# Half of the convolution's taps on GpSimd, root-mean-square norms by quarters, the last expert block written out

## What is computed

```python
a_lat = modulate(rms_norm(h_lat, g_pre_t), sh_t, sc_t)          # the same for ctx
z = split_columns(a @ w_in)                                      # conv, q, kv, k_rope, gmlp, gate
u = a_ * sigmoid(gate); u = depthwise_conv(u, dw, 31 taps) + db  # CONV_DIM = 512 channels
br_conv = silu(layer_norm(u)) @ w_conv_out
br_attn = attention(q, k, v) @ w_attn_out                        # 8 heads, 96 channels each
br_gmlp = chunk_gmlp(z_gmlp) @ w_gmlp_out
y = (g_conv * br_conv + g_attn * br_attn + g_gmlp * br_gmlp) @ w_out
h = h + gt_t * rms_norm(y, g_post_t)
f = swiglu(...)                      # layer 0: dense, width 2816
f = moe_swiglu(...)                  # layer 1: 8 experts of width 3584, top 2, 256 tokens
h = h + gt_f * rms_norm(f, g_post_f)
```

## Time and profile before

| | us |
|---|---|
| median of three runs | 2535.28 (2527.91 to 2539.51) |
| profiled execution | 2527.79, its span 2526.0 |
| blocks in the loop | 9, some 123.4 us each |

### The profile page before, as it was taken

One profiled execution on the slowest core, in us unless ns is written; L12 is line 12 of the kernel. 1 busy time (PEld: TensorE's weight loads), 2 busy tenths in 40 slices (PEclk: granted clock), 3 DMA queues, 4 the chain that ended last, 5 costly groups with the idle time before them and its releaser, 6 DMA issues.

```text
span 2526.0 us, 32159 instructions
## 1 busy us (share of the span) xinstructions
PE 2401.4 (95%) x12058; PEld 1943.0 (77%) x12058; DVE 1754.8 (69%) x1806; ACT 1385.4 (55%) x1455; POOL 46.0 (2%) x87
## 2 busy tenths in 40 slices
PE   7999999998999998877997999999999999999997
PEld 4757778875787885766996788888888888888886
DVE  4569753426333335778666989898989888888886
ACT  3456443334222223564656677777777777767675
POOL 0011000001000000000000000000000000000000
PEclk9989999999999999998998999999999999999998
DMA  7245223345434333313573999999999998989994
GB/s 278 73 133 188 67 84 109 109 162 197 134 109 134 108 99 126 105 38 105 167 250 139 371 346 368 354 355 360 360 349 367 348 367 340 376 338 373 341 373 175
DMA packets 104679, 579.36 MB, mean 229 GB/s; under 512 B 11920, under 2 KB 13840, under 8 KB 54800
## 3 DMA queue, kind: packets, MB, share of 16 engines
q1 hardware_dynamic: 93072, 536.21, 57.6%
q0 software_dynamic: 11520, 41.95, 4.8%
HBM read 577.06 MB, written 1.05 MB: 229 GB/s over the span
## 4 chain that ended last, share of the span: by engine, by line
PE 86%; DVE 8%; ACT 3%; issue 2%; DMA 1%; SPq 0%; DVEq 0%; ACTq 0%
PE bank L616 25%; PE bank L617 25%; PE bank L618 25%; DVE cacc L1549 2%; PE bank L691 2%; PE bank L1000 1%; PE bank L789 1%; DVE rstd L1490 1%; PE bank L1065 1%; PE bank L809 1%; PE bank L666 1%; DVE wlo L1470 1%; DVE t L1505 1%; ACT whi L1113 1%; DMA mod_s<-in_mod 1%
## 5 line engine op out<-in xcount | busy, mean ns | idle before, releaser
L1771 DVE TENSOR_TENSOR elo<-eraw,ehi 128x2048 fp32r<-128x2048 f32 x388 | 884.7, 2287 | 136.4 <-ACT ehi L1159 135.3
L1159 ACT CAST ehi<-eraw 128x2048 fp32r<-128x2048 f32 x388 | 741.2, 1914 | 254.0 <-PE bank L618 250.0
L1470 DVE TENSOR_TENSOR wlo<-raw,whi 128x1024 fp32r<-128x1024 f32 x220 | 269.5, 1225 | 286.8 <-ACT whi L1113 285.3
L616 PE MATMUL bank<-ah,whi 128*128 128x512 f32 (+1 forms) x1088 | 396.9, 365 | 19.7 <-DVE al L1511 9.3
L616 PE MATMUL bank<-ehi,xgh 128*128 128x512 f32 x1024 | 405.8, 396 | 1.5 <-DVE xgl L1777 1.2
L617 PE MATMUL bank<-elo,xgh 128*128 128x512 f32 x1024 | 399.7, 390 | 0.0
L618 PE MATMUL bank<-ehi,xgl 128*128 128x512 f32 x1024 | 399.3, 390 | 0.0
L617 PE MATMUL bank<-al,whi 128*128 128x512 f32 (+1 forms) x1088 | 390.0, 358 | 0.0
L618 PE MATMUL bank<-ah,wlo 128*128 128x512 f32 (+1 forms) x1088 | 389.9, 358 | 0.0
L1113 ACT CAST whi<-raw 128x1024 fp32r<-128x1024 f32 x220 | 229.2, 1042 | 118.9 <-PE bank L618 118.8
L616 PEld LDWEIGHTS bank<-ah,whi 128*128 128x128 f32 x1088 | 208.5, 192 | 57.5 <-issue 17.8
(11 more groups left out here) (270 smaller groups left out, 2766.2 us busy)
## 6 DMA issues: line engine op xcount, KB each, us to landing
eraw<-in_moe SPq DMA_DIRECT2D x388, 1024.0 KB, 4.9
raw<-in_dense SPq DMA_DIRECT2D x220, 512.0 KB, 3.5
mod_b<-in_mod POOLq DMA_DIRECT2D x48, 512.0 KB, 5.0
mod_a<-in_mod POOLq DMA_DIRECT2D x32, 512.0 KB, 4.3
mod_s<-in_mod SPq DMA_DIRECT2D x16, 512.0 KB, 12.9
hres<-in_xT SPq DMA_DIRECT2D x1, 2048.0 KB, 8.1
wsT<-in_wsT SPq DMA_DIRECT2D x2, 512.0 KB, 3.5
out_h<-hres SPq DMA_DIRECT2D x2, 512.0 KB, 3.0
```

The source lines that it names most:

```text
L616: pe.matmul(dst, wh, xh, start=first, stop=False, skip_group_check=True)
L1159: nc.scalar.copy(ehi[c % ESPLIT][:], eraw[c % ERAW][:]).then_inc(e_hi, 1)
L1470: dve.tensor_tensor(wlo[c % SPLIT][:], raw[c % RAW][:], whi[c % SPLIT][:].bitcast(F32), ALU.subtract).then_inc(w_lo, 1)
L1771: dve.tensor_tensor(elo[c % ESPLIT][:], eraw[c % ERAW][:], ehi[c % ESPLIT][:].bitcast(F32), ALU.subtract).then_inc(e_lo, 1)
```

## The change

**Taps.** The channel tiles 2 and 3 move to GpSimd, in both layers. For each tap it makes the product of the shifted input and the tap in a tile `tapp` and adds it to `cacc`: product 2, product 3, addition 2, addition 3. `tapp` lies over a part that `uk` and `uv` read, so from the second tap on it waits for `uv`. VectorE keeps tiles 0 and 1, one tap a unit in layer 0 and two in layer 1. PE waits for each half's sums by their own semaphore. GpSimd's loads of `mod_a` move to SyncE.

**Norms.** `add_squares` makes four matmuls of 32 output rows, each over a quarter of the tokens, so the sums lie in 32 rows each and 128 (or 64) columns; root and reciprocal work on these; `spread_roots` brings them by four matmuls with one column of `sel8` into the 128 rows and 512 columns of a PSUM bank `RB`, from which the multiplications read. The norms over the query, key and value channels, the convolution and the gMLP stay as they were.

**Experts.** The loop runs `n_iter` - 1 times on every engine; the last block follows as straight code without gather, `a` and `g` of q = 7, and without the splits and loads for them and for what would follow.

The core of the diff; the same replacements at the other norms, and the loop bodies of ScalarE and VectorE, which become functions in the same way, are left out:

```diff
@@ tables
+DVE_TILES = 2
 TAPS_CA = (5, 5, 5, 5)
-TAPS_UNIT = (2, 3)
+TAPS_UNIT = (1, 2)
+LAST_STEPS = [_s for _s in STEPS if _s[0] != "gather" and not (_s[0] in ("a", "g") and _s[1] == NB)]
+LAST_CHUNKS = [(*_s, _p) for _s in LAST_STEPS for _p in range(parts_of(_s[0]))]
@@ places
+        tapp = place("tapp", [P, 2, 2, LAT], F32, gm0 + 10240)
-        niter_i = place("niter_i", [P, 1], I32)
+        niter_i = place("niter_i", [P, 2], I32)
@@ sync
+                if c == CHUNK[("uk", 0)]:
+                    sp.wait_ge(mod_used, MOD_START)
+                    for i in range(MOD_A):
+                        sp.dma_start(mod_a[i][:], A["mod"][MOD_START + i]).then_inc(moda_landed[i], 16)
+                if c == CHUNK[("gv", 0, 2)]:
+
+                    for i in range(MOD_A, (VECS - 2) * KD):
+                        sp.wait_ge(mod_used, MOD_START + i - MOD_A + 1)
+                        sp.dma_start(mod_a[i % MOD_A][:], A["mod"][MOD_START + i]
+                                     ).then_inc(moda_landed[i % MOD_A], 16)
 ...
-            n_iter = sp.value_load(niter_i[0:1, 0:1], min_val=BLOCKS_MIN, max_val=BLOCKS_MAX)
-            with sp.Fori(0, n_iter) as it:
+            n_last = sp.value_load(niter_i[0:1, 1:2], min_val=BLOCKS_MIN - 1, max_val=BLOCKS_MAX - 1)
+            with sp.Fori(0, n_last) as it:
 ...
-            sp.wait_ge(e_lo, n_iter * EN + (EPRE + ERAW))
+            this = sp.value_load(ids_i[0:1, bass.ds(n_last, 1)], min_val=0, max_val=EXPERTS - 1)
+            for m in range(ERAW, EN_LAST):
+                sp.wait_ge(e_lo, n_last * EN + (EPRE + m - ERAW + 1))
+                fetch(A["moe"][bass.ds(this, 1)], stored(ECHUNKS.index(LAST_CHUNKS[m])), EPRE + m)
+
+            sp.wait_ge(e_lo, n_last * EN + (EPRE + EN_LAST))
@@ gpsimd
-            for i in range((VECS - 2) * KD):
-                pool.wait_ge(mod_used, MOD_START + max(i - MOD_A + 1, 0))
-                pool.dma_start(mod_a[i % MOD_A][:], A["mod"][MOD_START + i]).then_inc(moda_landed[i % MOD_A], 16)
+            tap_made = [0]
+
+            def taps(L):
+
+                ns = live(L) // LAT
+
+                def acc(i):
+                    return cacc[:, i, 0:ns * LAT].rearrange("p (s t) -> p s t", s=ns)
+
+                def product(t, i):
+                    src = up[:, i, 0:ns, t:t + LAT]
+                    w = p_(L, "conv_dw", TAPS * i + t)
+                    if t == 0:
+                        taken(pool, ("ca", L, i))
+                        pool.tensor_scalar(acc(i), src, w, p_(L, "conv_db", i), ALU.mult, ALU.add
+                                           ).then_inc(tap_done[i], 1)
+                    else:
+                        if (t, i) == (1, DVE_TILES):
+                            pool.wait_ge(chunk_used, CHUNK[("uv", L)] + 1)
+                        pool.wait_ge(tap_done[i], (TAPS - 1) * L + t)
+                        pool.tensor_scalar(tapp[:, i % 2, 0:ns, :], src, w, None, ALU.mult).then_inc(tap_made_sem, 1)
+                        tap_made[0] += 1
+
+                def addition(t, i, made):
+                    pool.wait_ge(tap_made_sem, made)
+                    pool.tensor_tensor(acc(i), acc(i), tapp[:, i % 2, 0:ns, :], ALU.add
+                                       ).then_inc(tap_done[i] if t < TAPS - 1 else conv_sum_pool, 1)
+
+                for t in range(TAPS):
+                    made = {}
+                    for i in range(DVE_TILES, 4):
+                        product(t, i)
+                        made[i] = tap_made[0]
+                    if t:
+                        for i in range(DVE_TILES, 4):
+                            addition(t, i, made[i])
+
+            taps(0)
 ...
+            taps(1)
@@ tensor
+            def add_squares(x, ntok, first, last):
+
+                w = ntok // 4
+                for j in range(4):
+                    mm = pe.matmul(STAT[32 * j:32 * j + 32, 0:w], ones[:, 0:32], x[:, j * w:(j + 1) * w],
+                                   start=first, stop=last, skip_group_check=True)
+                return mm
+
+            def spread_roots(ntok):
+
+                w = ntok // 4
+                pe.wait_ge(rs_ready, n.next(rs_ready))
+                for j in range(4):
+                    mm = pe.matmul(RB[:, j * w:(j + 1) * w], sel8[:, 2 * j:2 * j + 1].broadcast_to([P, P]),
+                                   rstd[:, 0:w], start=True, stop=True, skip_group_check=True)
+                mm.then_inc(rb_psum, 1)
 ...
                     for k in range(KD):
                         mod_chunk()
+                        if k == KD // 2:
+                            spread_roots(TOK)
                     stat_bank()
                     for k in range(KD):
                         pe.wait_ge(sq_ready, n.next(sq_ready))
-                        mm = pe.matmul(STAT[:], ones[:], t16[:, k, :], start=(k == 0), stop=(k == KD - 1),
-                                       skip_group_check=True)
+                        mm = add_squares(t16[:, k, :], TOK, k == 0, k == KD - 1)
                         if k == KD - 1:
                             mm.then_inc(sumsq_psum, 1)
                         mod_chunk()
                     n.next(sumsq_psum)
+                    spread_roots(TOK)
 ...
-                    pe.wait_ge(conv_sum, 4 * L + k + 1)
+                    if k < DVE_TILES:
+                        pe.wait_ge(conv_sum, DVE_TILES * L + k + 1)
+                    else:
+                        pe.wait_ge(conv_sum_pool, (4 - DVE_TILES) * L + k - DVE_TILES + 1)
 ...
-            with pe.Fori(0, n_iter) as it:
+            def iteration(it, steps):
                 c = EPRE
-                for kind, q, half in STEPS:
+                for kind, q, half in steps:
 ...
+            with pe.Fori(0, n_last) as it:
+                iteration(it, STEPS)
+            iteration(n_last, LAST_STEPS)
@@ scalar
+            def root_quarters(ntok):
+                w = ntok // 4
+                act.wait_ge(sumsq_psum, n.next(sumsq_psum))
+                nc.scalar.activation(std[:, 0:w], STAT[:, 0:w], ACT.Sqrt, bias=eps[:, 0:1], scale=1.0 / D
+                                     ).then_inc(std_ready, 1)
 ...
+            def round_next(it, c, steps):
+                if steps is STEPS or c < EPRE + EN_LAST:
+                    round_e(it, c)
@@ vector
+            def invert_quarters(ntok):
+
+                dve.wait_ge(std_ready, n.next(std_ready))
+                dve.reciprocal(rstd[:, 0:ntok // 4], std[:, 0:ntok // 4]).then_inc(rs_ready, 1)
+                dve.wait_ge(rb_psum, n.next(rb_psum))
 ...
-                    chain(dve.tensor_tensor(y[:, k, 0:ntok], y[:, k, 0:ntok], rstd[:, 0:ntok], ALU.mult))
+                    chain(dve.tensor_tensor(y[:, k, 0:ntok], y[:, k, 0:ntok], RB[:, 0:ntok], ALU.mult))
 ...
-                    taps_left.append([L, i, 0])
+                    if i < DVE_TILES:
+                        taps_left.append([L, i, 0])
 ...
-            dve.tensor_copy(niter_i[:], before[:, 16:17]).then_inc(niter_ready, 1)
+            chain(dve.tensor_copy(niter_i[:, 0:1], before[:, 16:17]))
+            dve.tensor_scalar(niter_i[:, 1:2], before[:, 16:17], 1.0, None, ALU.subtract).then_inc(niter_ready, 1)
```

More of the change, by code:

```diff
@@ L100 @@
 EN = 6 * NB
+EN_LAST = len(LAST_CHUNKS)
 ERAW = 6
@@ L659, in stat_bank, with sum_squares @@
                     pe.wait_ge(std_ready, n.n[sumsq_psum])
-            def sum_squares(nk, src, ntok):
-                stat_bank()
+            def add_squares(x, ntok, first, last):
[11 more added lines that the diff above has]
+                mm.then_inc(rb_psum, 1)
+            def sum_squares(nk, src, ntok, quarters=False):
+                stat_bank()
+                if quarters:
+                    for k in range(nk):
+                        pe.wait_ge(sq_ready, n.next(sq_ready))
+                        mm = add_squares(src(k), ntok, k == 0, k == nk - 1)
+                    mm.then_inc(sumsq_psum, 1)
+                    n.next(sumsq_psum)
+                    return
                 for k in range(nk):
@@ L1175, in _ @@
                     copy_rows(0)
-                    root(TOK, 1.0 / D, 0)
+                    root_quarters(TOK)
                     copy_rows(1)
@@ L1343, in _ @@
                 n.next(ysq_used, 1)
-                root(nq, 1.0 / D, 0)
+                root_quarters(nq)
                 if L:
@@ L1424, in _, with iteration @@
             n_iter = act.value_load(niter_i[0:1, 0:1], min_val=BLOCKS_MIN, max_val=BLOCKS_MAX)
-            with act.Fori(0, n_iter) as it:
+            n_last = act.value_load(niter_i[0:1, 1:2], min_val=BLOCKS_MIN - 1, max_val=BLOCKS_MAX - 1)
+            def round_next(it, c, steps):
+                if steps is STEPS or c < EPRE + EN_LAST:
+                    round_e(it, c)
+            def iteration(it, steps):
                 c = EPRE
-                for kind, q, half in STEPS:
+                for kind, q, half in steps:
                     if (kind, half) == ("scatter", 1):
```

(9 more changed lines are left out.)

70 lines of the change are left out of this document (43 added, 27 removed).

## The result

| | before | changed |
|---|---|---|
| median of five runs, us | 2535.28 (2527.91 to 2539.51) | 2546.87 (2546.43 to 2549.60) |
| profiled execution, span | 2526.0 | 2547.8 |

The changed kernel is slower by half a per cent: ratio 1.0053, 95% interval 1.0033 to 1.0073. I had forecast 2507, which is faster. Rival (b), GpSimd at the slower bound, said 2549.

What follows compares the result with a forecast made beforehand. TensorE, busy 95%, was taken as the bound, so cuts pay where it does less or stands. Norms -18.0, last block -16.2, taps +6 gave -28: 2500 us profiled, 2507 as median; range 2470 to 2560.

Steps and rivals of the forecast that it cites:

- Rival (b): Convolution taps: GpSimd at its slower bound, a pair 2.45 us, done at 334 and 1201; total 2549 us; chance 0.18.
- norms: Quarter norms in the layers and at the start: shorter sums, roots and reciprocals, less added spreading; -18.0 us, from -10 to -23.
- last block: Ninth expert block written out, without gather, dead products and unused weight split: -16.2 us, from -10 to -18.
- taps: Convolution taps moved to GpSimd: done at 304 in layer 0 and 1188 in layer 1, together +6 us.
- the price of GpSimd's pair: One tap's product and addition on GpSimd: 1.95 us at 512 columns, bounds 1.3 and 2.65; 1.18 at 256.
- The turns: VectorE's two-SBUF-operand instructions exclude GpSimd's for their whole length, all added to GpSimd: 42 us layer 0, 29 layer 1.
- fewer taps: VectorE's row beside GpSimd: the saving from its fewer taps, 0.7 us a unit, is eaten by its turns of waiting.
- bare norms: Four 512-token norms, at the end of layer 0's mixer and between the layers: -1.8 us each, together -7.2.
- The sums in PE's row: Layer 0's output projection and last feed-forward group: seven sums of squares each, 14 x 0.52 = 7.3 us saved.
- Layer 1's two norms at 256 tokens: Layer 1's norm chains: -0.3 us each, -0.6 together; seven sums there save another 0.9.
- the start: Eight squares at the kernel's start shrink by some 5 us, weights may still be landing: -2 taken, between 0 and -5.
- the uncovered turn: Last expert block: transpose, copies and hand-overs ahead of the last down-projections, 2.1 us instead of 11.6, giving -9.5.

Runs made afterwards that it cites:

- experiment 1: The changed kernel with all taps back on VectorE, quarter norms and written-out last block kept: 2498.31 us, ratio 0.9866 to the kernel before.
- experiment 3: The kernel before with only the last expert block written out: 2518.92 us, ratio 0.9946 to the kernel before.
- experiment 6: The changed kernel with GpSimd's product written as product and addition of constant 0: 2506.55 us, ratio 0.9883 to the kernel before.
- experiment 4: The changed kernel with VectorE's taps 1 to 29 of each of its two tiles left out: 2395.36 us, with eight expert blocks instead of nine.
- experiment 2: The changed kernel with one channel tile on GpSimd instead of two, VectorE at two and three taps a unit: 2518.74 us, ratio 0.9936 to the kernel before.
- experiment 7: The changed kernel with one tile on GpSimd instead of two, VectorE at one and two taps a unit: 2505.28 us, ratio 0.9884 to the kernel before.
- experiment 5: As experiment 4, but GpSimd's product in layer 0 changes its form every five taps; product 1.55 us, with addition of zero 0.69; no total time given.
- experiment 10: Experiment 1 with 16 of 31 taps of one layer 1 tile on GpSimd, cheap form, behind attention: 2500.35 us, ratio 0.9861 to the kernel before.

## Why the prediction was wrong

| term of the sum | forecast | measured |
|---|---|---|
| norms | -18.0 | -12.9 by the fixed points (experiment 1), some -20 by medians |
| last block | -16.2 | -17.2 (experiment 3), -17.9 (experiment 1), some -14 by medians |
| taps | +6 | +52.6 by the fixed points, some +47 by medians |
| sum | -28 | +21.8 between the two traces, +11.6 between the medians |

Two of the three terms held. **The step that failed is the price of GpSimd's pair.** I bounded it from a memset by the number of streams, 1.3 to 2.65 us, and took 1.95. Alone it is 2.77, outside the 1.7 to 2.2 that the prediction allowed itself (0.91 + 0.70 = 1.61 at 256 columns, where the upper bound was 1.5). The addition, 1.23, was near my 1.10; the product, with fewer streams, was the dear one, 1.54 for 0.85. A bound by streams can't see that a form of an instruction has a price of its own. The forecast's middle fits a form that the change doesn't use, 0.69 + 1.24 = 1.93, and with it experiment 6 came to 2507, the forecast. That is luck in part, since the forecast held no loss in attention. Since 0.1 us a pair is 6 us in layer 0, the error of 0.82 is 49 us there.

**The turns** were costed at their full length, 42 us in layer 0, all of it on GpSimd. GpSimd took 188 us from 144.7 to 332.7, 22 more than 60 x 2.77 (12 of them by VectorE's taps, experiment 4), and VectorE's taps in that stretch grew by 42 x 0.27 = 11. So the exclusion that the Trainium skill states ("SBUF — State Buffer", section "Who interferes with whom") shows in kind, but GpSimd paid about half of the length that I had put on it, and a part fell on VectorE. That part I had called eaten by fewer taps. It is not: it stands on the path ahead of each query. With GpSimd at work beside them layer 1's scores took 11 to 14 us more in the traces of experiments 2, 4, 6 and 7 and of the changed kernel (20 in experiment 5), with the dear form and the cheap one, at a lower granted clock. What brings that clock down stays open.

**Rival (b)** put GpSimd's end at 334 and the cost of layer 0 at +34 (332.7, +32.8), with a faster pair and larger turns than there were. Its +14 for layer 1 was right in size and not in kind: of the 13.9 us between first score and last sum, 10.8 are attention, and 3.1 what the longer wait leaves after VectorE's lighter row.

**The norms** hold in the chain. Each pair of bare norms gave 6.1 and 6.0 us, not 3.6. Behind the first of each pair stand eight steps of PE, a sum and a modulation chunk; they were 1.63 us apart and are now 1.51, VectorE's pace, and the first of them had been the slowest (1.83 and 1.54). I had counted only the last sum. The sums in PE's row gave less, 2.1 and 1.0 us for seven instead of 3.6 each: the four matmuls take the 0.34 I took, but PE's row loses 0.1 us ahead of them and 0.1 behind. In `out` the distance from sum to sum fell from 6.34 only to 6.02. Layer 1's two norms at 256 tokens and its sums gave nothing (+0.9, forecast -1.5), the start nothing: the chain goes through the transfer of `mod_s`, landed at 31.9. Another 1.3 us were lost ahead of layer 1's first score, which I didn't follow up.

**The last block** came as summed: the uncovered turn was 1.5 us of waiting (2.3 between the two groups of products, forecast 2.1), and PE waited for no weight.

## What to carry to other kernels

Before work moves to an engine whose arithmetic no trace shows, measure the very form of instruction that will be used, and a neighbouring form beside it; a price worked out by streams is not a bound. An engine that works beside VectorE costs where VectorE's short rows stand between TensorE and its next work, and a longer pause of TensorE can come with a lower granted clock that costs several times its length, though not each time. A trace is one execution: look where it lies among the others before its differences are taken for those of the kernels. Judge the parts of a change apart: here two of the three were worth 1.3%, and the third hid them.

## What the runs showed of the hardware

- GpSimd, 128x512 float32: a product with a per-channel factor 1.55 us, with the addition of a per-channel value behind it 0.76, of a constant 0.69; addition of two tensors 1.24. At 256 columns 0.91 for the product in one operation and 0.70 for the addition.
- A VectorE instruction with two operands in SBUF can take longer beside GpSimd by about one instruction of it: 0.42 us became 1.20, next to additions of 0.71. The other way round, GpSimd's first tap took 0.76 us with VectorE quiet (experiment 4) and 1.83 in the changed kernel.
- Three added pauses of 0.84 us brought TensorE's mean granted clock in layer 1's attention from 0.94 to 0.73 and came with 14.4 us more, in one execution; another kernel's trace shows 0.76 there without them (experiment 10). After 30 us of standing (granted 0.50) it had 0.85 in the next 36 us, where the kernel before had 0.95 in the same work.
